# Sixteen places for the expert weights in place of fourteen, and a normalisation whose gain is applied before its scale is known

## What is computed

```
for e in range(N_EXPERTS):                      # 32
    h = silu(t @ w_exp_gate[e]) * (t @ w_exp_up[e])
    y = y + combine[:, e:e + 1] * (h @ w_exp_down[e])
```

## Time and profile before

| | |
|---|---|
| median of the runs | 1592.61 us |
| the profiled execution: its own time | 1588.47 us |
| its span, first to last instruction | 1586.7 us |
| TensorE busy | 1489.1 us, 94% |
| VectorE, ScalarE, GpSimd busy | 717.8, 574.3, 414.8 us |
| granted TensorE clock, mean | 0.989 of full |
| DMA | 381.10 MB, 240 GB/s over the span |
| share of the chain that ended last | TensorE 67%, DMA 20%, VectorE 4% |

### The profile page before, as it was taken

How to read it: one execution, slowest core, us unless ns; L and a number is a source line. 1 busy time by engine, 2 the same in 40 slices (tenths; PEclk the granted TensorE clock), 3 DMA queues, 4 the chain that set the end, 5 groups by cost and what they waited for, 6 DMA issues and landing times.

```text
span 1586.7 us, 23298 instructions
## 1 busy us (share of the span) xinstructions
PE 1489.1 (94%) x9430; PEld 1027.2 (65%) x9430; DVE 717.8 (45%) x1294; ACT 574.3 (36%) x779; POOL 414.8 (26%) x316
## 2 busy tenths in 40 slices
PE   5899999999999799999999999789999899999997
PEld 2788888888667544434434334368788678878786
DVE  2678887575535832112111111245523644343673
ACT  2522425454333312212112112334344355464553
POOL 0000000010000101000000000139887686757554
PEclk9999999999999999999999999999999999999999
DMA  8633224434778989999999999846556353434332
GB/s 309 205 127 105 80 80 162 133 107 162 260 249 293 414 320 420 421 422 422 422 422 422 422 422 422 327 139 221 163 183 211 118 180 108 137 129 133 133 111 89
DMA packets 120877, 381.10 MB, mean 240 GB/s; under 512 B 9302, under 2 KB 11134, under 8 KB 96222
## 3 DMA queue, kind: packets, MB, share of 16 engines
q1 hardware_dynamic: 120798, 380.02, 63.8%
HBM read 378.95 MB, written 1.05 MB: 239 GB/s over the span
## 4 chain that ended last, share of the span: by engine, by line
PE 67%; DMA 20%; DVE 4%; ACT 3%; POOL 3%; issue 2%; SPq 1%; POOLq 0%; DVEq 0%; ACTq 0%
DMA arena<-in_w_exp_up 18%; PE ps L786 12%; PE ps L793 12%; PE ps L787 11%; PE ps L1207 7%; PE ps L968 3%; PE ps L967 3%; PE ps L974 3%; POOL w_lo L2441 3%; PE ps L1219 2%; PE ps L867 2%; ACT w_hi L2523 1%; PE ps L887 1%; PE ps L1370 1%; PE ps L1230 1%
## 5 line engine op out<-in xcount | busy, mean ns | idle before, releaser
L2441 POOL TENSOR_TENSOR w_lo<-ring,w_hi 128x512 fp32r<-128x512 f32 x280 | 373.7, 1375 | 126.9 <-ACT w_hi L2523 115.3
L2523 ACT ACTIVATE w_hi<-ring 128x2048 fp32r<-128x2048 f32 x130 | 246.7, 1912 | 306.4 <-PE ps L793 137.5
L786 PE MATMUL ps<-w_hi,xt_hi 128*128 128x512 f32 x512 | 202.0, 395 | 0.3 <-ACT w_hi L2523 0.3
L787 PE MATMUL ps<-w_hi,xt_lo 128*128 128x512 f32 x480 | 187.0, 390 | 0.0
L1542 DVE TENSOR_TENSOR w_lo<-ring,w_hi 128x2048 fp32r<-128x2048 f32 x60 | 138.2, 2304 | 88.6 <-ACT w_hi L2523 88.3
L786 PE MATMUL ps<-w_hi,yt_hi 128*128 128x512 f32 x352 | 139.0, 395 | 2.8 <-issue 2.2
L793 PE MATMUL ps<-w_lo,xt_hi 128*128 128x512 f32 x512 | 127.3, 391 | 5.1 <-POOL w_lo L2441 5.1
L1207 PE MATMUL ps<-arena 128*32 128x512 f32 x1056 | 118.9, 593 | 11.1 <-DMA arena<-in_w_exp_up 11.0
L2096 DVE TENSOR_SCALAR selT<-ps 128x256 fp32r<-128x256 f32 x32 | 13.6, 425 | 248.3 <-ACT arena L2854 248.3
L1207 PE MATMUL ps<-ring,arena 128*32 128x512 f32 x992 | 111.7, 593 | 11.9 <-DMA ring<-in_w_exp_up 10.9
L2441 POOL TENSOR_TENSOR w_lo<-ring,w_hi_ahead 128x512 fp32r<-128x512 f32 x8 | 9.9, 1275 | 422.4 <-ACT w_hi_ahead L2842 420.9
(11 more groups left out here) (323 smaller groups left out, 2372.4 us busy)
## 6 DMA issues: line engine op xcount, KB each, us to landing
ring<-in_w_in SPq DMA_DIRECT2D x40, 1024.0 KB, 5.1
ring<-in_b_w_in SPq DMA_DIRECT2D x40, 1024.0 KB, 5.1
arena<-in_w_exp_gate SPq DMA_DIRECT2D x33, 1024.0 KB, 23.0
arena<-in_w_exp_up SPq DMA_DIRECT2D x33, 1024.0 KB, 25.0
arena<-in_w_exp_down SPq DMA_DIRECT2D x32, 1024.0 KB, 23.3
ring<-in_w_exp_down SPq DMA_DIRECT2D x32, 1024.0 KB, 23.3
ring<-in_w_exp_gate SPq DMA_DIRECT2D x31, 1024.0 KB, 23.0
ring<-in_w_exp_up SPq DMA_DIRECT2D x31, 1024.0 KB, 25.0
```

The source lines that it names most:

```text
L786: pe.matmul(o[:, tt, :], hi[:, k, x_], w[:, c, :], start=(bias is None and j == 0 and c == 0), stop=False)
L787: pe.matmul(o[:, tt, :], lo[:, k, x_], w[:, c, :], start=False, stop=False)
L2441: ins = pool.tensor_tensor(w_lo2[:, slots_of[n], k, :], ring[:, slots_of[n], k, :], w[:, k, :].bitcast(F32), ALU.subtract)
L2523: act.activation(part_of(n)[1][:, :, :], ring[:, slots_of[n]], ACT.Copy).then_inc(S("w_hi_full"), 1)
```

## The change

1. `EXTRA = 4`: four one-time places instead of two, for k = 0 to 3 of expert 2. The two new ones lie where the transposed expert input and the rest of `h` were (`o_XT2`, `o_XT + 2048`). SP waits for `routed` before it issues the third and for `h_left` before the fourth. The four share two semaphores.
2. `second_pair`: as unit k of expert 0 is used up, SP issues for its slot k = 0 to 3 of expert 4 and k = 4, 5 of expert 2. `third_pair` issues only k = 4, 5 of expert 4 and all of expert 5.
3. The three gain rows are issued behind `third_pair`, not ahead of it; their wait is gone.
4. Ahead of the experts: k = 0, 1, 2 of expert 1 are issued together behind unit `("mix", 1, 1)`, k = 4, 5 behind `("tail", 6, 0)`.
5. The norm behind a final product: the gain is multiplied in before the scale is known. The first 512 columns of both tiles are done ahead, the last 512 of a tile while GpSimd makes its power. Behind the power one `scalar_tensor_tensor` of 1024 columns multiplies by the scale and adds. This is done for `h1` and for the output.

```diff
+EXTRA = 4
...
-            fills.append(slots_of.count(slots_of[n]))
+            fills.append(slots_of.count(slots_of[n]) - (n >= first["a"] and slots_of[n] in EVEN_SLOTS[:EXTRA]))
...
-        extra = [carve(UC, W, on=on)[0] for on in (o_S, o_S + 2048)]
+        extra = [carve(UC, W, on=on)[0] for on in (o_S + 2048, o_S, o_XT2, o_XT + 2048)]
...
-            if second and not odd and k < 2:
+            if second and not odd and k < EXTRA:
...
-                if n in (at_unit["tail", 6, 0], at_unit["tail", 6, 1], at_unit["tail", 7, 0]):
-
-                    sp.wait_ge(S("unit_done"), end_of("ret", 1, 4))
-                    expert_unit(0, 1, n - at_unit["tail", 6, 0], 0)
-                if n == at_unit["tail", 7, 0]:
+                if n == at_unit["mix", 1, 1]:
+
+                    sp.wait_ge(S("retT_turned"), 4)
+                    for k in range(3):
+                        expert_unit(0, 1, k, 0)
+                if n == at_unit["tail", 6, 0]:
...
                 for k in range(2):
                     extra_unit(k)
+                sp.wait_ge(S("routed"), NT)
+                extra_unit(2)
+                sp.wait_ge(S("h_left"), 4)
+                extra_unit(3)
+                for k in range(6):
+                    sp.wait_ge(S("unit_done"), n_before + k + 1)
+                    expert_unit(4 if k < EXTRA else 2, 0, k, 0)
+                for k in range(6):
+                    sp.wait_ge(S("unit_done"), n_before + 6 + k + 1)
+                    expert_unit(2, 1, k, 0)
+
+            def third_pair():
+
                 for odd in range(2):
-                    for k in range(2 * (1 - odd), 6):
-                        sp.wait_ge(S("unit_done"), n_before + 6 * odd + k + 1)
-                        expert_unit(2, odd, k, 0)
-
-            def third_pair():
-
-                for odd in range(2):
-                    for k in range(6):
-                        if odd or k >= 2:
-                            sp.wait_ge(S("unit_done"), n_before + 12 + 6 * odd + k + 1)
+                    for k in range(0 if odd else EXTRA, 6):
+                        sp.wait_ge(S("unit_done"), n_before + 12 + 6 * odd + k + 1)
                         expert_unit(4, odd, k, 0)
...
                     second_pair()
-
-                    sp.wait_ge(S("h_left"), 4)
+                    third_pair()
                     for v, name in ((ln2_g, "ln2_g"), (ln2_b, "ln2_b"), (pre0, "norm_pre_2")):
                         sp.dma_start(v, a[name][0:1].broadcast_to([P, D])).then_inc(S("load_gains"), 16)
-                    third_pair()
...
+            def scale_and_product(tt, i, done, gain, key):
+                dve.wait_ge(S("squared"), done + tt + 1)
+                dve.tensor_tensor(ms[:, tt:tt + 1], squares[:, i, tt:tt + 1], squares[:, i + 1, tt:tt + 1], ALU.add).then_inc(S("power_asked"), 1)
+                link(dve.tensor_tensor(h1[:, tt, W:D], buf(key)[:, tt, :], gain[:, 1, :], ALU.mult))
+                power_ready()
+
             for tt in range(NT):
-                product_scale(tt, 1, 4)
+                link(dve.tensor_tensor(h1[:, tt, 0:W], y2[:, tt, 0:W], gain1[:, 0, :], ALU.mult))
+            for tt in range(NT):
+                scale_and_product(tt, 1, 4, gain1, ("a_out", 1))
                 if tt:
                     rest_tokens("bT", 0)
-                link(normed_product(tt, h1, ("a_out", 1), gain1))
                 settle()
-                dve.tensor_tensor(h1[:, tt, :], h1[:, tt, :], x_pre1[:, tt, :], ALU.add).then_inc(S("b_in_ready"), 1)
+                dve.scalar_tensor_tensor(h1[:, tt, :], h1[:, tt, :], rstd[:, tt:tt + 1], x_pre1[:, tt, :], ALU.mult, ALU.add).then_inc(S("b_in_ready"), 1)
...
             for tt in range(NT):
-                product_scale(tt, 1, 10)
-                link(normed_product(tt, y2, ("b_out", 1), post1))
+                link(dve.tensor_tensor(h1[:, tt, 0:W], y2[:, tt, 0:W], post1[:, 0, :], ALU.mult))
+            for tt in range(NT):
+                scale_and_product(tt, 1, 10, post1, ("b_out", 1))
                 settle()
-                dve.tensor_tensor(x[:, tt, :], x[:, tt, :], y2[:, tt, :], ALU.add).then_inc(S("out_ready"), 1)
+                dve.scalar_tensor_tensor(x[:, tt, :], h1[:, tt, :], rstd[:, tt:tt + 1], x[:, tt, :], ALU.mult, ALU.add).then_inc(S("out_ready"), 1)
```

More of the change, by code:

```diff
@@ L612, in extra_unit @@
             def extra_unit(k):
-                sp.dma_start(extra[k].rearrange("p k c -> p (k c)"), moe_src(PARTS[k][0], 2, PARTS[k][1])).then_inc(S("extra_full%d" % k), 16)
+                sp.dma_start(extra[k].rearrange("p k c -> p (k c)"), moe_src(PARTS[k][0], 2, PARTS[k][1])).then_inc(S("extra_full%d" % (k // 2)), 16)
             for n in range(n_before):
@@ L1188, in arrived @@
                 s_ = expert_slot(odd, k)
-                if order == "second" and not odd and k < 2:
-                    pe.wait_ge(S("extra_full%d" % k), 16)
+                if order == "second" and not odd and k < EXTRA:
+                    pe.wait_ge(S("extra_full%d" % (k // 2)), 32)
                 else:
-                    missed = s_ in EVEN_SLOTS[:2] and order != "first"
+                    missed = s_ in EVEN_SLOTS[:EXTRA] and order != "first" and not (rd and s_ < RING2)
                     pe.wait_ge(full_of(s_, rd), e * 8 + 16 * (filled_times(s_, rd) + 1 - missed))
@@ L2239, in part_sums @@
                 settle()
[L2241 to L2244, removed]
             def normed_product(tt, dst, key, gain):
```

## The result

The changed kernel takes **1581.59 us**, the median of five runs (1578.64 to 1583.68), against 1591.3 us for the kernel before beside it (1586.22 to 1593.86): ratio 0.9942, 95% interval 0.9925 to 0.9958. By the ratio that is 9.2 us less (6.7 to 11.9). The profiled execution took 1578.64 us with a span of 1576.8 us, 9.9 us under the span of before; mean granted clock 0.993.

A forecast was written before the change was run, and what follows sets the result against it. TensorE was taken to carry the chain nearly everywhere, the DMA queue the experts' stage from 686 us. 2.6 + 0.4 + 2.5 = 5.5 us off 1592.61 gave 1587.1 us, own range 1585 to 1589.4, 8 in 10 within 1582.5 to 1590.5.

The forecast's parts named there:

- Part 2: Ahead of the experts: five units of expert 1 moved ahead fill the queue's hole of 510 to 515 us; 0 us.
- Part 1: Experts' stage: two more one-time places and the gain rows moved end the stage 2.6 us earlier, bounds -0.7 and 5.9.
- The second hole: Experts' stage: SP has nothing to issue before 594.69 us, so the queue is idle again for 5 us or so.
- restarts without loss: Experts' stage, half of a rival: the emptied queue loses nothing on restart, 5.9 us there; chance 0.19 with its other half.
- doesn't do what it says in the experts' stage: Rival: second dry spell and gain rows eat the two units, 0 in that stage, 2.9 us in all, 1589.7; chance 0.15.
- the slower rival: Experts' stage: every request to the emptied queue pays, 12.0 us slower, 1604.6; chance 0.04.
- the first rival: Queue restarts without loss, or clock stays up at mixer b: 8.8, 8.1 or both 11.4 us, 1581.2 to 1584.5; chance 0.19.
- Part 3: Norm toward mixer b: tile 1.5 us earlier, mostly not passed on; 0.4 us gained, no change by the clock.
- the bound that I had named: Mixer b: three product groups stay at full clock, 2.6 us, with the 0.4 a gain of 3.0.
- GpSimd's run did not shut the new instruction out: Mixer b rival: GpSimd's remainders shut the new instruction out, tile 3.6 us later, 1.5 us gained in all, 1591.1; chance 0.07.
- Part 4: Last norm: one instruction behind the power for each tile in place of three; 2.5 us, bounds 2.2 and 2.7.

The follow-up runs named there:

- e1: The changed kernel with the five units of expert 1 issued where they were before; 1584.64 against 1589.67 us, 0.9967.
- e5: The kernel before with only the new norm, at both places; 0.9995.
- e6: The kernel before with only the further one-time places, SP's new order and the gain rows behind; units not moved, old norm; 0.9973.
- e1_again: The changed kernel with the five units of expert 1 not moved, run a second time; 0.9959.
- after_again: The changed kernel once more, in the next batch; 1581.01 against 1590.67 us, 0.9950.
- e2: The kernel before with only the five units of expert 1 moved ahead; 0.9994.
- e3: The kernel before with 18 filler products on TensorE ahead of its wait for `h_ready`, no transfer moved; 0.9998.
- e4: The changed kernel with the three gain rows issued in the queue's new idle stretch; 1576.57 us, 0.9914.
- e7: The changed kernel with gain rows in the idle stretch and 12 filler products in TensorE's wait for `xt2_lo`, at MLP and mixer b starts; 0.9915.
- e8: The changed kernel with the five units not moved and 18 filler products ahead of the first turn of the experts' input; 0.9950.
- e9: The changed kernel with gain rows in the idle stretch, fillers at MLP and mixer b starts, and the old norm toward mixer b; 0.9921.

## Why the prediction was wrong, and where it was right

**The step that failed is Part 2: "TensorE stands idle there waiting for `h_ready`. I cost it at 0."** I priced the move in the queue alone. There I saw that the three units of `tail` would come later, and that TensorE had idle time to take that up. Both held. For the third of the `tail` units, issued at 518.4 us, after has:

```profile
L600 SPq DMA_DIRECT2D ring<-in_w_ada x1: 379/379/379, 518.4 to 518.4; - x1
...
  PE ps L893: 1.7, 1
...
DMA to landing us min/median/max: 8.9/8.9/8.9
```

It lands at 527.3 us, after 8.9 us (5.8 before), and TensorE waits 1.67 us for it. I had said one or two us later; it is three. What I left unpriced is what that idle time did. Where it stood in one piece of 2.31 us, the granted clock afterwards was 0.62, and sixteen products took 3.63 us. Where other work divided or filled it, the clock stayed at 1.00 and they took 1.94. All five traces in which nothing lay in that gap (before, e1, e5, e6, e1_again) have S1 from 31.14 to 31.17. All eight in which products of a late unit or a filler lay in it (after, after_again, e2, e3, e4, e7, e8, e9) have 29.01 to 29.21. e3 and e8 show the cause without a transfer moved ahead. That the late unit acts by dividing the gap is how I read the timeline; a kernel that delays that unit alone was not run.

Why the 2.1 us reach the end: the queue's last start is a request that TensorE makes, when it has used up expert 2's down unit. From the first expert product to that request it is 39.60 us before (594.69 - 555.09) and 39.58 after (592.36 - 552.78). TensorE sets the pace up to there, so the queue starts 2.1 us sooner as well. Part 1 took 594.69 us from the old trace as a fixed time, where it is the first expert product plus 39.6 us; that holds in e1, e4 and e5 too.

**Part 1, the places: right in mechanism, a little small.** The second hole opened where it was forecast. The restart cost 6.7 - 5.1 = 1.6 in the first landing, which I had put at nothing, and 18.4 - 17.4 = 1.0 in the seven steps, where I took 3.3: 2.6 in all, so part of the nearness is luck. The rows behind cost 3.8: norm_pre, issued at 609.1, lands after 12.2 us, at 621.3. Over all traces S2 is 455.2 with the old places (four traces), 451.8 with the new (six) and 448.3 with the rows in the hole (three): 3.4 us where the forecast had 2.6. Neither "restarts without loss" (5.9) nor "doesn't do what it says in the experts' stage" (0) came, and the slower rival would have needed 1.5 us a request; the sum over eight was 2.6. The measured time lies in the range of the first rival (1581.2 to 1584.5), but neither of its two mechanisms was at work in that trace.

**Part 3, the norm toward mixer b: right in kind, size open.** The instruction met one remainder: 2.24 us in place of 1.28 alone, 1.0 more, as charged. Counted from the event at which B begins, the tile is ready after 4.83 us (6.57 before), 1.7 sooner for 1.5 forecast, and `xt2_lo` begins after 8.98 (9.47 before), 0.5 sooner. The low clock moved one group on: with the old norm the first b group took 1.92 to 2.05 us in all five traces, with the new 1.15 to 1.17 in all eight. How long it stayed low behind that differs by execution, and in e4 it never fell (B 27.00, 2.4 less than before; the bound that I had named was 3.0). B is 28.50 on the mean of seven traces with the new norm and no filler, 29.01 on four with the old: 0.5 for 0.4, but the ranges (27.00 to 29.70, 28.75 to 29.38) overlap, so the agreement may be luck. GpSimd's run did not shut the new instruction out.

The Trainium skill, "SBUF — State Buffer", section "Who interferes with whom", has such a pair shut each other out for the length of one instruction, and I read that as a wait for one remainder at most. For L2270 (2.24 us, one remainder) the trace agrees. For L2252 it does not: it took 8.85 us beside a run of remainders that ended at 1219.89, and ended 1.1 us behind it. In e5 the same addition took 8.72 us and the two behind it 2.35 together. Both cases happen in one execution, and the rule so read has no place for the second.

**Part 4, the last norm: right, a little small.** E is 11.75 on the mean of the traces with the old norm (11.73 to 11.78) and 9.00 with the new (8.95 to 9.04): 2.75 for 2.5. The product from PSUM ends with GpSimd's power (1571.78 + 0.61 = 1572.39 us against 1571.86 + 0.54 = 1572.40), so the 0.1 a tile that I charged did not come.

**The sum again**, with the measured terms: 2.1 + 3.4 + 0.5 + 2.75 = 8.75 us, ratio 0.9945, inside 0.9925 to 0.9958. The profiled pair shows 9.9; most of the rest is 0.24 at the start and 0.73 at the start of the MLP, which is 55.3 to 57.3 long from one execution to the next whatever was changed. Of the 5.5 us between 1587.1 and 1581.59, 3.25 are these terms and 1.3 is the base: I subtracted from 1592.61, and the kernel before beside the changed one took 1591.3. The last 1.0 is within what the interval leaves open.

What stays open: the size of the norm's part at mixer b, why the first `tail` product comes anywhere from 523.6 to 528.4 us (523.94 and 528.43 in e1 and e1_again, which are the same program), and why at mixer b the clock fell in some executions of the same lines and not in e4.

**The best version** is e4, 1576.57 us, 0.9914 [0.9900, 0.9929]: the change with the rows in the hole. The filler of e7 adds nothing that can be measured. The intervals of e4 and of the changed kernel overlap by a little (0.9925 to 0.9929); the three kernels with the rows in the hole have 0.9914, 0.9915 and 0.9921, the two timings of the changed kernel 0.9942 and 0.9950.

## What to carry to other kernels

Before an idle stretch of TensorE is costed at nothing, look at the granted clock behind it: an idle time is a cover for late work, and it can also be what makes the next products run at half speed (3.63 us against 1.94 here). Look in more than one execution: ahead of the experts the clock fell in the same kernels every time, at mixer b it did not. When a transfer queue has run dry and starts again on a consumer's request, take that request's time relative to the consumer's start, so that whatever starts the consumer sooner is passed on whole. Loads that nobody needs soon belong in the stretch in which the queue is dry anyway, and not behind it.

## What the runs showed of the hardware that was not expected

- Ahead of the experts one idle time of 2.31 us on TensorE was followed by a granted clock of 0.62 and then 0.53; 1.67 and 0.36 us with 1.06 us of products between were followed by 1.00. Eighteen products of no use, 2.13 us, did the same. It was decided the same way in all 13 traces. At the start of mixer b it was not: behind the same idle times of 1.16 and 1.95 us four products took 1.93 us (after), 2.07 (after_again) and 1.20 (e4).
- A queue asked again after being dry landed its first unit of 1 MB 6.7 us later (5.1 in the kernel before), and seven further units with few waiting took 18.4 us, at 2.49 us each it would be 17.4.
- A VectorE addition of 1024 columns beside back-to-back remainders on GpSimd took 8.5 to 9.2 us in all 13 traces, about 1.2 in their absence, and ended 1.1 us behind the run in both traces looked at (before, after), while another VectorE instruction that began just behind the start of such a run got through in 2.24.
